# Forgetting attention in a two-layer fp32 encoder: mask folded into the row maximum, values in two stacked passes, splits and normalisation on GpSimd

## The reference, cut to what matters

```
D=1024, SEQ=512, DEPTH=2, 16 heads of 64, D_FF=2816
for layer 0 (forgetting attention) and layer 1 (sliding-window GQA):
    h += 0.5 * swiglu(rms_norm(h))
    h += mixer(rms_norm(h))
    h += 0.5 * swiglu(rms_norm(h))
return rms_norm(h)

def fox_mixer(x):                       # layer 0's mixer
    q, k, v, f_logit = split(x @ w_in)
    c = cumsum(log_sigmoid(f_logit + b_f))
    s = q k^T * 64**-0.5 + c_t - c_s    # per head, 512 x 512
    s = where(t >= s, s, -inf)
    p = softmax(s)
    return (p v) @ w_o
```

## Time and profile before

| | |
|---|---|
| median of 3 runs | 1895.15 us (1893.53 to 1895.56) |
| span of the profiled execution | 1890.3 us |
| PE busy | 1856.6 us, 98% |
| DVE busy | 933.2 us, 49% |
| ACT busy | 720.6 us, 38% |
| POOL busy | 23.6 us, 1% |

### The profile page before, as it was taken

How to read it: one execution, slowest core, us unless ns; L and a number is a source line. 1 busy time by engine, 2 the same in 40 slices (tenths; PEclk the granted TensorE clock), 3 DMA queues, 4 the chain that set the end, 5 groups by cost and what they waited for, 6 DMA issues and landing times.

```text
span 1890.3 us, 23832 instructions
## 1 busy us (share of the span) xinstructions
PE 1856.6 (98%) x8632; PEld 1523.7 (81%) x8632; DVE 933.2 (49%) x1335; ACT 720.6 (38%) x1168; POOL 23.6 (1%) x43
## 2 busy tenths in 40 slices
PE   8999999999998999999999999999998999999998
PEld 6888888877776888888888888888877788888886
DVE  6444444356886544444344444444378644444333
ACT  4223223237775432232233232223269532322322
POOL 0000000000000000000000000000000000000000
PEclk9999999999999999999999999999999999999999
DMA  4322223332111223222333222223321222222332
GB/s 157 100 90 99 97 84 109 111 100 67 57 46 45 100 90 100 92 97 82 107 108 110 94 100 97 89 91 105 119 67 46 79 92 98 100 92 88 98 103 86
DMA packets 55206, 174.31 MB, mean 92 GB/s; under 512 B 6640, under 2 KB 8688, under 8 KB 55152
## 3 DMA queue, kind: packets, MB, share of 16 engines
q1 hardware_dynamic: 55008, 173.57, 28.2%
q10 hardware_dynamic: 144, 0.03, 0.0%
HBM read 171.48 MB, written 2.10 MB: 92 GB/s over the span
## 4 chain that ended last, share of the span: by engine, by line
PE 93%; ACT 3%; DVE 2%; issue 1%; DMA 0%; POOL 0%; SPq 0%; DVEq 0%; ACTq 0%; POOLq 0%
PE bank L413 90%; PE bank L618 1%; PE bank L631 1%; ACT scratch L1114 1%; ACT w_hi L849 1%; DVE w_lo L1186 0%; PE bank L730 0%; ACT wide_hi L1070 0%; ACT wide_hi L1062 0%; DMA scratch<-x_dram 0%; PE bank L439 0%; ACT wide_hi L1016 0%; DVE wide_lo L1393 0%; PE bank L433 0%; DVE acc L1207 0%
## 5 line engine op out<-in xcount | busy, mean ns | idle before, releaser
L1186 DVE TENSOR_TENSOR w_lo<-raw,w_hi 128x1024 fp32r<-128x1024 f32 (+1 forms) x355 | 404.9, 1141 | 849.1 <-ACT w_hi L849 847.9
L849 ACT ACTIVATE w_hi<-raw 128x1024 fp32r<-128x1024 f32 (+1 forms) x355 | 352.3, 992 | 874.6 <-PE bank L413 869.9
L413 PE MATMUL bank<-u_hi,w_hi 128*128 128x512 f32 x1624 | 644.2, 397 | 0.3 <-DVE w_lo L1186 0.3
L413 PE MATMUL bank<-u_lo,w_hi 128*128 128x512 f32 x1624 | 633.2, 390 | 0.0
L413 PE MATMUL bank<-u_hi,w_lo 128*128 128x512 f32 x1624 | 633.2, 390 | 0.0
L413 PEld LDWEIGHTS bank<-u_hi,w_lo 128*128 128x128 f32 x1624 | 304.6, 188 | 64.5
L413 PEld LDWEIGHTS bank<-u_hi,w_hi 128*128 128x128 f32 x1624 | 305.1, 188 | 62.1 <-issue 1.4
L413 PEld LDWEIGHTS bank<-u_lo,w_hi 128*128 128x128 f32 x1624 | 305.1, 188 | 61.2 <-issue 1.2
L413 PE MATMUL bank<-wide_hi,w_hi 128*128 128x512 f32 x832 | 325.3, 391 | 0.7 <-issue 0.4
L413 PE MATMUL bank<-wide_lo,w_hi 128*128 128x512 f32 x832 | 323.8, 389 | 0.0
L413 PE MATMUL bank<-wide_hi,w_lo 128*128 128x512 f32 x832 | 323.8, 389 | 0.0
(11 more groups left out here) (138 smaller groups left out, 1111.9 us busy)
## 6 DMA issues: line engine op xcount, KB each, us to landing
raw<-ffn_in_dram SPq DMA_DIRECT2D x176, 512.0 KB, 3.2
raw<-ffn_out_dram SPq DMA_DIRECT2D x128, 384.0 KB, 3.0
raw<-mix_w_dram SPq DMA_DIRECT2D x51, 512.0 KB, 3.2
y_dram<-raw SPq DMA_DIRECT2D x8, 256.0 KB, 2.9
scratch<-x_dram SPq DMA_DIRECT2D x3, 512.0 KB, 6.6
x_last<-x_dram SPq DMA_DIRECT2D x1, 512.0 KB, 8.5
sink<-sinks_dram SPq DMA_DIRECT2D x2, 2.0 KB, 7.3
gain<-gains_dram ACTq DMA_DIRECT2D x1, 28.0 KB, 4.0
```

The source lines that it names most:

```text
L413: mm = pe.matmul(out, a, b, start=first and k == 0, stop=last and k == n - 1)
L849: act.activation(w_hi[:, slot, 0:cols], raw[:, (base + r) % RAW, 0:cols], ACT.Copy)\
L1186: dve.tensor_tensor(w_lo[:, s, 0:cols], raw[:, r, 0:cols], f32(w_hi[:, s, 0:cols]), ALU.subtract).then_inc(w_ready, 1)
```

## The change

1. **Mask in the row maximum.** The 64 bf16 mask matmuls go. DVE's row maximum becomes one instruction that adds the scores and the mask, negates, keeps the minimum and writes the masked, negated scores back into PSUM; the exponential then has scale -1. The compiler makes two DVE instructions of it, the main one and a one-column one. The mask is now fp32, in `sq`, and is written by POOL at the stage's start.
2. **Values in two stacked passes.** V is stored with its hi and lo parts side by side, 64 columns each. One pass multiplies P's hi part with both (128 output rows), one multiplies P's lo part with V's hi part (64 rows). The lower half of the result has to be added to the upper: ACT copies it to `o_parts`, DVE adds the two halves.
3. **To GpSimd.** The hi and lo parts of o, the lo parts of q and k, and the normalisation of P move to POOL, in one hand-written order.

```diff
+        o_parts = x_last[:, :].rearrange("p (k c) -> p k c", k=2)
-        causal = sb("causal", [P, P], BF16)
+        causal = sq[:, 0, :]
+        def v_heads(t, first, count):
+            part = (wide_hi, wide_lo)[t // 2]
+            a = V_AT + t % 2 * 2 * D + first * 2 * DH
+            return part[:, a:a + count * 2 * DH].rearrange("p (h s c) -> p h s c", s=2, c=DH)
...
+            def fox_project_lo(count, j, is_q):
+                pool.wait_ge(qk_hi_ready, count)
+                for par in range(2):
...
+                    last = pool.tensor_tensor(to, scaled[own, :], f32(wide_hi[own, at:at + SEQ]), ALU.subtract)
+                last.then_inc(qk_ready, 1)
+            def fox_output(t):
+                rows = slice(64 * (t % 2), 64 * (t % 2) + 64)
+                a = O_AT + t // 2 * SEQ
+                pool.wait_ge(o_summed, t + 1)
+                pool.tensor_copy(wide_hi[rows, a:a + SEQ], o_parts[rows, 1, :]).then_inc(o_hi_ready, 1)
+                pool.wait_ge(o_hi_ready, t + 1)
+                pool.tensor_tensor(wide_lo[rows, a:a + SEQ], o_parts[rows, 1, :], f32(wide_hi[rows, a:a + SEQ]),
+                                   ALU.subtract).then_inc(o_ready, 1)
+            def fox():
...
+                for t in range(HEADS + 1):
+                    j, b = t // 2, t % 2
+                    if t + 1 < HEADS:
+                        fox_pick(t + 1)
+                    if j + 1 < PAIRS:
+                        fox_project_lo(t + 3, j + 1, b == 0)
+                    if t:
+                        fox_output(t - 1)
+                    if t < HEADS:
+                        pool.wait_ge(rsum_ready, t + 1)
+                        if t:
+                            pool.wait_ge(o_ready, t)
+                        pool.wait_ge(qk_ready, min(t + 3, 2 * PAIRS))
+                        for i in ORDER:
+                            part = prob[t % 2][:, FOX_P_AT[i]:FOX_P_AT[i] + FOX_KEYS[i]]
+                            last = pool.tensor_scalar(part, part, rsum[:, t % 2, i:i + 1], None, ALU.mult)
+                        last.then_inc(p_ready, 1)
...
-                    pe.matmul(out[:, nk - P:nk], ident_bf[:, :], causal[:, :],
-                              start=False, stop=True).then_inc(scored, 1)
...
-                    products(bank[7][0:DH, kb * P:SEQ],
-                             [(wide(v_at, v_at + DH), wide(p_at, p_at + cols))], kb == 0, kb == TB - 1)\
-                        .then_inc(pv_done, 1)
+                    out = bank[7][:, kb * P:SEQ]
+                    if kb == 0:
+                        pe.matmul(out, v, wide_hi[:, p_at:p_at + cols], start=True, stop=False)
+                    mm = pe.matmul(out[0:DH, :], v[:, 0, :], wide_lo[:, p_at:p_at + cols], start=False, stop=False)
+                    if kb > 0:
+                        mm = pe.matmul(out, v, wide_hi[:, p_at:p_at + cols], start=False, stop=kb == TB - 1)
+                    mm.then_inc(pv_done, 1)
...
-                        act.activation(wide_hi[64 * par:64 * par + 64, O_AT + jo * SEQ:O_AT + (jo + 1) * SEQ],
-                                       bank[7][0:DH, :], ACT.Copy).then_inc(o_hi_ready, 1)
+                        if t >= 2:
+                            act.wait_ge(o_summed, t - 1)
+                        act.activation(o_parts[0:DH, 0, :], bank[7][DH:2 * DH, :], ACT.Copy).then_inc(o_lower, 1)
...
-                        dve.tensor_reduce(nmax[:, b, i:i + 1],
-                                          bank[FOX_BANK[i]][:, FOX_BANK_AT[i]:FOX_BANK_AT[i] + FOX_KEYS[i]],
-                                          AX_X, ALU.max, negate=True).then_inc(nmax_ready, 1)
+                        dve.tensor_tensor_reduce(out=s_i, in0=s_i, in1=causal[:, SEQ - FOX_KEYS[i]:SEQ], scale=-1.0,
+                                                 scalar=-MASKED, op0=ALU.add, op1=ALU.min,
+                                                 accum_out=nmax[:, b, i:i + 1]).then_inc(nmax_ready, 1)
...
+                        dve.wait_ge(o_lower, t)
...
+                        dve.tensor_tensor(o_parts[rows, 1, :], bank[7][0:DH, :], o_parts[0:DH, 0, :], ALU.add)\
+                           .then_inc(o_summed, 1)
```

More of the change, by code:

```diff
@@ L207, in build @@
         pv_done = sem("pv_done")
+        o_lower = sem("o_lower")
+        o_summed = sem("o_summed")
         o_hi_ready = sem("o_hi_ready")
@@ L617, in score @@
                     for k, part in enumerate((wide_hi, wide_lo)):
-                        pe.matmul(out, part[:, q_at:q_at + P], part[:, k_at:k_at + nk], start=k == 0, stop=False)
-                    pe.matmul(out[:, nk - P:nk], ident_bf[:, :], causal[:, :],
-                              start=False, stop=True).then_inc(scored, 1)
+                        mm = pe.matmul(out, part[:, q_at:q_at + P], part[:, k_at:k_at + nk], start=k == 0, stop=k == 1)
+                    mm.then_inc(scored, 1)
                 def turn(t, kb):
@@ L1367, in project_scaled @@
                         dve.tensor_tensor(scaled, bank[1][:, :], rstd_row[:, :], ALU.mult).then_inc(qk_scaled, 1)
-                def project_lo(count, j, is_q):
-                    dve.wait_ge(qk_hi_ready, count)
-                    for par in range(2):
-                        own = slice(64 * par, 64 * par + 64)
-                        at = FOX_Q_AT[par][j % 2] if is_q else FOX_K_AT[par]
-                        to = wide_lo[own, at:at + SEQ] if is_q else wide_hi[beside(par), at:at + SEQ]
-                        last = dve.tensor_tensor(to, scaled[own, :], f32(wide_hi[own, at:at + SEQ]), ALU.subtract)
-                    last.then_inc(qk_ready, 1)
                 for k in range(2):
```

79 lines of the change are left out of this document (38 added, 41 removed).

## The result

| | before | the change |
|---|---|---|
| median | 1894.34 us (1893.33 to 1895.56, 4 runs) | 2007.16 us (2006.67 to 2008.33, 4 runs) |
| profiled execution, span | 1890.3 us | 2005.6 us |
| mean granted TensorE clock | 0.998 | 0.969 |

The ratio is 1.0595, 95% interval 1.0583 to 1.0607: 5.95% slower. The direction and the place were foreseen, the size was not: 46 us were forecast, 113 came, 32 us above the range's upper end. (The forecast was set on the 1895.15 us of three runs of before; the fourth run lowers that median to 1894.34.)

A forecast was written before the change was run, and what follows sets the result against it. PE, 98% busy, bounds the kernel before; after the change a loop through POOL's normalisation does. 2.83 us more in 13 iterations, 36.8, plus start, last iterations and end make 46.4 us: 1895.15 + 46.4 = 1941.5 us, range 1912 to 1975.

The forecast's parts named there:

- The loop: Attention iteration: t0, ACT's stretch, addition, output, normalisation, t0 sets the period, 13.10 us instead of 10.27.
- Term 5: POOL's normalisation of P in the loop: four instructions, 1280 columns at 0.84 ns, 1.81 us.
- twice the estimate, 3.62: Upper end for POOL's normalisation of P, used in the dear-POOL rival: 1977 us, chance 0.14.
- Term 1: ACT's copy of the head's output ends 7.40 us after t0, as today, since ACT has no gap.
- hand-overs: Five passes between or within engines in the loop, 0.05 us each: 0.25 us.
- the first iteration, the last two and the tail: Outside the 13 iterations: up to the first t0 +2.1 us, last two intervals +1.2 and +4.8, behind the last t0 +1.5.
- Term 8: POOL's output subtraction in the loop starts 1.11 us late, as DVE's weight split and POOL exclude each other.
- Term 4: POOL's two-operand subtraction of 64x512 for the output's lo part, in the loop: 1.04 us.
- Term 7: DVE's row maximum of blocks 0 and 1, between ACT's copies, adds 0.17 us to the loop.
- The faster rival: Attention: PE stays the bound and all of its 18 us saving comes, 1877 us; chance 0.03.

The follow-up runs named there:

- e1: The change with the normalisation of P back on DVE, ahead of its addition of o's halves: 1895.73 us, ratio 1.0005 to the kernel before.
- e10: The change with a plain copy in place of the normalisation (division left out) and 12 useless matmuls per head ahead of t0's wait: 1943.8 us, ratio 1.0258.
- e4: The change with four forms of POOL's normalisation in turn over the heads (pointer scalar, constant scalar, two-operand product, copy): 1990.85 us, a single execution.
- e3: The change with 20 useless matmuls per head ahead of t0's wait, to keep PE busy: 1983.22 us, ratio 1.0472.
- e5: The change with POOL's normalisation as a two-operand product, the reciprocal broadcast along the row: 1979.11 us, ratio 1.0445.
- e7: The change with normalisation and q's and k's lo parts back on DVE, only o's hi and lo parts on POOL: 1897.5 us, ratio 1.0014.
- e8: e7 with ACT's copy of P's block 2 moved ahead of the hi part of the next q or k: 1893.22 us, ratio 0.9998.
- e9: e1 with ACT's copy of P's block 2 moved ahead of the hi part of the next q or k: 1900.44 us, ratio 1.0022.
- e12: e8 with DVE's weight split moved behind the row maxima of blocks 3 and 2: 1900.16 us, ratio 1.0025.
- e2: The change with POOL's normalisation of head t ahead of the previous head's output instead of behind it: 1946.94 us, ratio 1.028.

## Why the prediction was right about the loop and wrong about its size

- **The loop** (t0, ACT, addition, output, normalisation, t0) was right: the same links in the same order, released by L415, and e1 gives back the whole loss when the last link goes. In e10, with both missed items near their forecast values, the loop has the forecast's length.
- **Term 5, the normalisation, is the step that failed first.** It was put at 1.81 us and took 4.27. It was priced from the cast's 0.84 ns per column as "one operand". The copy does cost that (e4), the scalar form three times as much. 2.46 us per iteration in 13 iterations are 32 us. The upper end, "twice the estimate, 3.62", was itself a multiple of the wrong row and lay below the 4.27 measured. No row of before showed this form; a bound for an unseen form should have held a per-column cost above that of the two-operand form.
- **Term 1, "ACT's copy ends at T+7.40 as today", failed second.** The copy ended at T+9.04. The term is true only while PE runs at the full clock behind `t0`. The forecast put 3 to 4 us of idling before each `t0`, but priced it as time alone. The granted clock was 0.50 at its end and in the 4.5 us behind it (e3, where PE does not idle so long: 1.6 us less per iteration, some 24 us in all). This was in neither the sum nor a rival, and the range had no room for it.
- **The total.** The two items and 0.14 us more of hand-overs make 4.07 us x 13 = 53 us; the first iteration, the last two and the tail were 16 us over their forecast. That is the 69 us between the 46 forecast and the 115 in the span. At the start the normalisation of head 0 takes 5.05 us instead of 1.81; but e10, with a copy there, still comes 6.2 us late to its first `t0` where 2.1 were forecast, so this part of the sum was too low for another reason too, the clock behind the first wait for k. e5 shows that 1.5 us less of the normalisation doesn't bring the clock back.
- **Term 8 (conflict) was right**, from one row in seven: the subtraction took 2.13 us where a split ran beside it, 1.29 us in iteration 14, which has none, and 1.28 to 1.29 in e7, e8 and e9, where it ran beside no split. In e12 it took 1.28 us beside a split at 516.76, and there it was the split that became longer (2.08). **Term 4** alone was 0.25 us too low, term 8 0.27 too high. The trace agrees with the rule in the Trainium skill (SBUF — State Buffer, "SBUF: two separate sides") that two such instructions exclude each other. By the same rule the one that starts first keeps the ports; this fits 541.92 and e12, but not the row at 389.50, where POOL started first and was the longer. DVE's TENSOR_SCALAR normalisation, which has one wide SBUF operand, lengthens too (e1, e9: 1.28 to 2.3 and 2.7 us); why, no run shows. The estimate of 1.12 us from the Trainium skill's figure (GPSIMD Engine Reference, "Performance versus the Vector engine") is nearer to the measured 1.29 than my 1.04.
- **Term 7 was nearly nothing**: the main instruction for 512 columns takes 0.69 us, the read-out of 0.14 us lies beside the next instruction, and in e3 the copy ends at T+7.35 with it.
- **The faster rival's premise**, that PE's 18 us come through once POOL doesn't hold it, fell as well: in e1, e7 and e8 PE waits for P's blocks instead. PE's 98% said nothing of how near the next chain was: in e8, the best of the open forms, the 15 intervals took 148.5 us against 150.8, so 0.15 of the 1.1 us per head arrived. The 1.1 itself was a little high: two masks between `s0` and `t1` were worth 0.14 us (0.60 us from 517.49 to 518.09 before, 0.46 us from 515.54 to 516.00 in e8), where 0.26 were counted. And what e8 gained up to the last `t0` was lost behind it.
- **What stays open:** in e8 the exact chain that sets the 10.1 us was read from its rows and not isolated. How long the idle time must be for the clock to fall was not varied on purpose. It fell behind waits of 5.3 us (the change) and of 0.55 to 1.28 us (e7, iteration 13), and in e4 it fell behind 2.5 us in one iteration and not in another. A form with the loop open and the last head's output left on DVE was not run.

## What to carry to other kernels

Before moving work to another engine, look for who will wait for it in the same iteration: a step that closes a loop costs its whole length, each time. Price an unseen instruction form with a bound that does not come from a simpler form, and where waits on TensorE are forecast, price the slower clock behind them as well. When an engine at 98% is relieved, read the second-latest chain before counting the saving, and read the stage's end too, where a chain that the loop hides has nothing to hide behind.

## What the runs showed of the hardware

- POOL, fp32, 128 rows, per column: copy 0.84 ns, two-operand product 1.67 ns, scalar multiplication 2.5 ns. A subtraction of 64x512 with fp32r output took 1.29 us.
- TensorE after 5.3 us of idling, in the change: granted clock 0.50, and 1.00 again after 4.5 us of work. In e2 after 2.5 us of idling the `t0` itself took 0.66 us and the clock fell behind it, to 0.50 from 504.3 to 506.3. In e7 it was 0.50 from 586 to 592, behind waits of 0.55, 0.70 and 1.28 us.
- POOL and DVE lengthen each other: POOL's cast 0.61 to 1.66 us, its subtraction 1.29 to 2.13, its normalisation 4.27 to 5.11, DVE's weight split 1.23 to 2.08, its normalisation 1.28 to 2.72.
